# A sixth buffer for weight sets in a Strassen feed-forward, and the remainders' subtractions moved from GpSimd to VectorE

## The reference

```python
gate, up = split(h @ ffn_w_in, 2)          # ffn_w_in: 1024 x 5632
f = (silu(gate) * up) @ ffn_w_out          # ffn_w_out: 2816 x 1024
h = layer_norm(alpha * h + f)              # alpha = 4 ** 0.25
```

## Time and profile before

| | us |
|---|---|
| median of three runs | 2912.92 (2907.91 to 2914.14) |
| the profiled execution | 2908.02 |
| its span | 2906.2 |
| TensorE busy | 2577.3 (89%) |
| VectorE busy | 1685.0 (58%) |
| GpSimd busy | 1082.5 (37%) |
| ScalarE busy | 801.3 (28%) |
| sets' sums on GpSimd, L905, per block | 150.7 and 151.1 (x105 each) |
| sets' remainders on GpSimd, L908, per block | 136.1 and 136.2 (x105 each) |
| sets' remainders on VectorE, L779, per block | 41.9 (x42 each) |

### The profile page before, as it was taken

One profiled execution on the slowest core, in us unless ns is written; L12 is line 12 of the kernel. 1 busy time (PEld: TensorE's weight loads), 2 busy tenths in 40 slices (PEclk: granted clock), 3 DMA queues, 4 the chain that ended last, 5 costly groups with the idle time before them and its releaser, 6 DMA issues. The chain is left out here.

```text
span 2906.2 us, 40422 instructions
## 1 busy us (share of the span) xinstructions
PE 2577.3 (89%) x12972; PEld 2133.7 (73%) x12972; DVE 1685.0 (58%) x2971; ACT 801.3 (28%) x1363; POOL 1082.5 (37%) x810
## 2 busy tenths in 40 slices
PE   6787889699999999968999999995969999999995
PEld 5676678577777777757888888885857777777774
DVE  8789437645444454482667766666565444444447
ACT  3224232322222222213222222222132322222220
POOL 3979201545554544501011111100155545554450
PEclk9887999899999999989999999997989999999998
DMA  4333222244344333412110111102224434343341
GB/s 135 94 102 91 75 87 88 62 126 116 108 115 119 112 101 101 131 58 57 30 37 22 36 36 36 29 7 73 87 58 123 120 108 119 113 118 101 101 121 60
DMA packets 392575, 248.25 MB, mean 85 GB/s; under 512 B 24352, under 2 KB 374688, under 8 KB 391584
## 3 DMA queue, kind: packets, MB, share of 16 engines
q1 hardware_dynamic: 392480, 247.02, 28.9%
HBM read 229.20 MB, written 17.76 MB: 85 GB/s over the span
## 5 line engine op out<-in xcount | busy, mean ns | idle before, releaser
L835 DVE TENSOR_TENSOR h<-h,ps 128x512 f32<-128x512 f32 x320 | 219.4, 686 | 179.0 <-PE ps L498 178.9
L1977 POOL TENSOR_TENSOR w_lo<-w_raw_plain,w_hi 128x1024 fp32r<-128x1024 f32 x38 | 91.7, 2420 | 562.0 <-ACT w_hi L62 562.0
L2005 PE MATMUL ps<-aT_hi,w_hi 128*128 128x512 f32 x640 | 257.1, 402 | 1.7 <-PEq L324 1.7
L2005 PE MATMUL ps<-aT_hi,w_lo 128*128 128x512 f32 x640 | 251.7, 393 | 0.0
L2005 PE MATMUL ps<-aT_lo,w_hi 128*128 128x512 f32 x640 | 250.2, 391 | 0.0
L468 PE MATMUL ps<-aT_hi,s5o_w_sets 128*128 128x512 f32 x672 | 221.5, 401 | 28.0 <-DVE s5o_w_sets L779 20.0
L468 PE MATMUL ps<-aT_hi,hgo_w_sets 128*128 128x512 f32 x672 | 220.5, 399 | 28.4 <-DVE hgo_w_sets L779 20.0
L905 POOL TENSOR_TENSOR hgo_w_sets_plain<-hgo_w_sets_plain 128x512 f32<-128x512 f32 x105 | 150.7, 1436 | 177.3 <-DMA hgo_w_sets_plain<-in_ffn_w_in_dram 177.3
L905 POOL TENSOR_TENSOR s5o_w_sets_plain<-s5o_w_sets_plain 128x512 f32<-128x512 f32 x105 | 151.1, 1439 | 114.7 <-DMA s5o_w_sets_plain<-in_ffn_w_in_dram 114.7
L908 POOL TENSOR_TENSOR s5o_w_sets<-s5o_w_sets_plain,s5o_w_sets 128x512 fp32r<-128x512 f32 x105 | 136.2, 1297 | 132.5 <-ACT s5o_w_sets L62 131.6
L908 POOL TENSOR_TENSOR hgo_w_sets<-hgo_w_sets_plain,hgo_w_sets 128x512 fp32r<-128x512 f32 x105 | 136.1, 1296 | 131.0 <-ACT hgo_w_sets L62 131.0
(11 more groups left out here) (382 smaller groups left out, 6243.0 us busy)
## 6 DMA issues: line engine op xcount, KB each, us to landing
s5o_w_sets_plain<-in_ffn_w_in_dram SPq DMA_DIRECT2D x210, 256.0 KB, 3.3
hgo_w_sets_plain<-in_ffn_w_in_dram SPq DMA_DIRECT2D x210, 256.0 KB, 3.3
w_raw_plain<-in_hg_w_in_dram SPq DMA_DIRECT2D x40, 512.0 KB, 3.9
s5o_w_raw<-in_ffn_w_out_dram SPq DMA_DIRECT2D x22, 512.0 KB, 4.7
hgo_w_raw<-in_ffn_w_out_dram SPq DMA_DIRECT2D x22, 512.0 KB, 4.7
s5o_w_sets_plain<-in_ffn_w_in_dram SPq DMA_DIRECT2D x84, 128.0 KB, 2.3
hgo_w_sets_plain<-in_ffn_w_in_dram SPq DMA_DIRECT2D x84, 128.0 KB, 2.3
h<-in_x_dram SPq DMA_DIRECT2D x4, 1024.0 KB, 8.7
```

The lines of the kernel that those rows point to most:

```text
L835: v.tensor_tensor(to, to, ps[:, 4 + m % 4, :], ALU.add).then_inc(S["out_acc"], 1)
L1977: g.tensor_tensor(w_lo[b][:, :, :], w_raw[b][:, :, :], w_hi[b][:, :, :].bitcast(F32), ALU.subtract).then_inc(E[f"w_lo_done{b}"], 1)
L2005: ins = t.matmul(ps[:, half, :], w[b][:, kk, :], x[:, kk, cols], start=(kk == 0 and q == 0), stop=(kk == KT - 1 and q == 2))
```

## The change

- `SLOTS` is 6 and `SLOT_AT` is pos modulo 6. The norm's rows of gamma and beta lie in slots 4 and 5, before in 0 and 1.
- GpSimd makes only the sums (`make_sum`). VectorE makes all 14 remainders of an iteration (`set_lo`), and TensorE waits on one counter.
- `w2_raw` is gone. Both row blocks of `ffn_w_out` are loaded by one transfer of 1 MB straight into the memory of `w2_lo`, and the remainder is written in place. This load waits for the outputs before, whose operand it overwrites; it stands ahead of the iteration's set loads on SyncE.
- The hand-written orders of ScalarE, VectorE and GpSimd follow: `set_lo` calls stand between merges and between pairs of accumulations, and `w2_split` comes later in the iteration.

The diff (some context left out, deep lines moved left by eight columns):

```diff
@@ -160 +160 @@
-SLOTS = 5
+SLOTS = 6
@@ -210 +210 @@
-    w2_raw = sb("w2_raw", [P, D])
-    g_row, b_row = (plain_slots[:, n, :, :].rearrange("p h c -> p (h c)") for n in range(2))
+    w2_plain = in_rows(k.plain[tag + "_w2_lo"])
+    g_row, b_row = (plain_slots[:, n, :, :].rearrange("p h c -> p (h c)") for n in (4, 5))
-"set_in0", "set_in1", "set_in2", "set_in3", "set_in4", "set_sum", "set_hi", "set_lo", "set_lo_dve",
+"set_in0", "set_in1", "set_in2", "set_in3", "set_in4", "set_in5", "set_sum", "set_hi", "set_lo",
@@ -242 +242 @@
+    FIRST = range(NP, 2 * NP)
-    SLOT_AT = [0, 1, 2, 3, 4, 0, 1, 2, 3, 4, 0, 1, 2, 3]
+    SLOT_AT = [n % SLOTS for n in range(2 * NP)]
...
@@ -348 +345 @@
-    def load_w2(f):
-        if not (isinstance(f, int) and f == 0):
-            s.wait_ge(S["w2_lo"], f)
-            carry(s, f)
-        s.dma_start(w2_raw[:, :], w_out_v[:, ds(f, 1), :].rearrange("p f d -> p (f d)")
-                    ).then_inc(S["w2_loaded"], 16)
+    def load_w2(i):
+        if isinstance(i, int) and i == 0:
+            s.wait_ge(S["tile"], 2 * NT)
+        else:
+            s.wait_ge(S["out_tile"], i * NOUT)
+            carry(s, i)
+        s.dma_start(w2_plain, w_out_v[:, ds(2 * i, FG), :]).then_inc(S["w2_loaded"], 16)
@@ -368 +366 @@
     for half in range(2):
         tiles = slice(4 * half, 4 * half + 4)
         s.dma_start(h[:, tiles, :], residual_v[:, tiles, :]).then_inc(S[f"back{half}"], 16)
-    load_w2(0)
     s.wait_ge(S["w_lo"], 12)
-    for pos in range(NP, NP + 3):
+    for pos in FIRST[:3]:
         load_set(-1, pos)
     s.wait_ge(S["normed"], NT)
-    for pos in range(NP + 3, 2 * NP):
+    for pos in FIRST[3:]:
         load_set(-1, pos)
-    for pos in range(5):
+    load_w2(0)
+    for pos in range(SLOTS):
         load_set(0, pos)
 
     def body(i):
-        load_set(i, 5)
-        load_w2(2 * i + 1)
-        for pos in range(6, 2 * NP):
+        if not (isinstance(i, int) and i == 0):
+            load_w2(i)
+        for pos in range(SLOTS, 2 * NP):
             load_set(i, pos)
-        load_w2(2 * i + 2)
         if not (isinstance(i, int) and i == LAST - 1):
-            for pos in range(5):
+            for pos in range(SLOTS):
                 load_set(i + 1, pos)
 
     body(0)
@@ -397 +394 @@
-    load_w2(NF_LAST)
+    load_w2(LAST)
@@ -452 +449 @@
-            if IS_SUM[r]:
-                t.wait_ge(S["set_lo"], sums_to(i, pos))
-            else:
-                t.wait_ge(S["set_lo_dve"], plain_to(i, pos))
+            t.wait_ge(S["set_lo"], index(i, pos) + 1)
@@ -618 +612 @@
         keep_pair(pair)
     set_hi(-1, 10)
     set_hi(-1, 11)
+    set_hi(-1, 12)
     keep(0, 0)
     keep(0, 1)
-    set_hi(-1, 12)
+    set_hi(-1, 13)
     keep(0, 2)
-    set_hi(-1, 13)
     silu_late(0)
     set_hi(0, 0)
     silu_early(0)
-    for pos in range(1, 5):
+    for pos in range(1, SLOTS):
         set_hi(0, pos)
 
     def w2_split(i, q):
-        a.wait_ge(S["w2_loaded"], 16 * (2 * i + q + 1))
+        a.wait_ge(S["w2_loaded"], 16 * (i + 1))
         carry(a, i)
-        if isinstance(i, int) and i == 0:
-            a.wait_ge(S["tile"], 2 * NT)
-        else:
-            a.wait_ge(S["out_tile"], i * NOUT)
-            carry(a, i)
-        split_hi(a, w2_hi[:, q, :], w2_raw[:, :]).then_inc(S["w2_hi"], 1)
+        split_hi(a, w2_hi[:, q, :], w2_plain[:, q, :]).then_inc(S["w2_hi"], 1)
 
     def body(i):
         hidden_hi(2 * i, 0, i)
-        w2_split(i, 0)
         keep(2 * i + 1, 0)
         keep(2 * i + 1, 1)
-        set_hi(i, 5)
+        set_hi(i, 6)
+        set_hi(i, 7)
         keep(2 * i + 1, 2)
-        set_hi(i, 6)
-        w2_split(i, 1)
+        set_hi(i, 8)
         silu_late(2 * i + 1)
-        set_hi(i, 7)
+        set_hi(i, 9)
         silu_early(2 * i + 1)
-        set_hi(i, 8)
-        set_hi(i, 9)
+        w2_split(i, 0)
+        set_hi(i, 10)
         hidden_hi(2 * i + 1, 1, i)
+        set_hi(i, 11)
         keep(2 * i + 2, 0)
         keep(2 * i + 2, 1)
-        for pos in range(10, 13):
-            set_hi(i, pos)
+        w2_split(i, 1)
+        set_hi(i, 12)
+        set_hi(i, 13)
         keep(2 * i + 2, 2)
-        set_hi(i, 13)
         silu_late(2 * i + 2)
-        final = isinstance(i, int) and i == LAST - 1
-        if not final:
-            set_hi(i + 1, 0)
         silu_early(2 * i + 2)
-        if not final:
-            for pos in range(1, 5):
+        if not (isinstance(i, int) and i == LAST - 1):
+            for pos in range(SLOTS):
                 set_hi(i + 1, pos)
 
     body(0)
@@ -776 +762 @@
-        v.tensor_tensor(lo, plain_rows(pos)[1], hi.bitcast(F32), ALU.subtract).then_inc(S["set_lo_dve"], 1)
+        v.tensor_tensor(lo, plain_rows(pos)[1], hi.bitcast(F32), ALU.subtract).then_inc(S["set_lo"], 1)
-        v.tensor_tensor(w2_lo[:, q, :], w2_raw[:, :], w2_hi[:, q, :].bitcast(F32), ALU.subtract
+        v.tensor_tensor(w2_lo[:, q, :], w2_plain[:, q, :], w2_hi[:, q, :].bitcast(F32), ALU.subtract
@@ -844 +830 @@
         split_piece(1, kk)
     for n in range(NT):
         add_projection(0, n)
+    for pos in range(7, 10):
+        set_lo(-1, pos)
     for pair in range(PAIRS):
         for n in (2 * pair, 2 * pair + 1):
             add_projection(1, n)
@@ -851 +839 @@
         if pair >= 1:
             keep_pair(pair - 1)
     keep_pair(PAIRS - 1)
-    set_lo(-1, 10)
-    set_lo(-1, 11)
-    merge_steps(0, range(1, 11))
-    set_lo(0, 3)
-    set_lo(0, 4)
+    for pos in range(10, 13):
+        set_lo(-1, pos)
+    merge_steps(0, range(1, 5))
+    set_lo(-1, 13)
+    merge_steps(0, range(5, 11))
+    for pos in range(SLOTS):
+        set_lo(0, pos)
 
     def body(i):
+        merge_steps(2 * i + 1, range(1, 3))
+        set_lo(i, 6)
+        merge_steps(2 * i + 1, range(3, 5))
+        set_lo(i, 7)
+        merge_steps(2 * i + 1, range(5, 7))
+        set_lo(i, 8)
+        merge(2 * i + 1, 7)
+        set_lo(i, 9)
+        merge_steps(2 * i + 1, range(8, 10))
+        set_lo(i, 10)
+        merge(2 * i + 1, 10)
         split_w2(i, 0)
-        merge_steps(2 * i + 1, range(1, 5))
+        set_lo(i, 11)
+        merge_steps(2 * i + 2, range(1, 3))
+        set_lo(i, 12)
+        merge_steps(2 * i + 2, range(3, 5))
+        set_lo(i, 13)
         split_w2(i, 1)
-        merge_steps(2 * i + 1, range(5, 11))
-        set_lo(i, 10)
-        merge(2 * i + 2, 1)
-        set_lo(i, 11)
-        merge_steps(2 * i + 2, range(2, 11))
-        accumulate(i, slice(0, 4))
-        if not (isinstance(i, int) and i == LAST - 1):
-            set_lo(i + 1, 3)
-            set_lo(i + 1, 4)
-        accumulate(i, slice(4, NT))
+        merge_steps(2 * i + 2, range(5, 11))
+        final = isinstance(i, int) and i == LAST - 1
+        for two in range(PAIRS):
+            accumulate(i, slice(2 * two, 2 * two + 2))
+            if not final and two:
+                set_lo(i + 1, 2 * two - 2)
+                set_lo(i + 1, 2 * two - 1)
 
     body(0)
     with v.Fori(1, LAST - 1) as i:
@@ -897 +899 @@
-    def make_set(i, pos):
+    def make_sum(i, pos):
-        (hi, lo), (one, other) = set_rows(pos), plain_rows(pos)
+        one, other = plain_rows(pos)
-        g.wait_ge(S["set_hi"], index(i, pos) + 1)
-        carry(g, i)
-        g.tensor_tensor(lo, other, hi.bitcast(F32), ALU.subtract).then_inc(S["set_lo"], 1)
@@ -920 +919 @@
             g.tensor_tensor(hid_lo[:, q, HALF_COLS[half]], act_out[half][:, :],
                             hid_hi[:, q, HALF_COLS[half]].bitcast(F32), ALU.subtract).then_inc(S["hid"], 1)
 
-    for pos in range(NP, NP + 3):
-        make_set(-1, pos)
+    for pos in (7, 8, 9):
+        make_sum(-1, pos)
     for pair in range(PAIRS):
         pair_lo(pair)
-    make_set(-1, 12)
-    make_set(-1, 13)
-    for pos in range(3):
-        make_set(0, pos)
+    make_sum(-1, 12)
+    make_sum(-1, 13)
+    for pos in (0, 1, 2, 5):
+        make_sum(0, pos)
 
     def body(i):
         hidden_lo(2 * i, 0)
-        for pos in (5, 6, 7, 8, 9):
-            make_set(i, pos)
+        for pos in (6, 7, 8, 9):
+            make_sum(i, pos)
         hidden_lo(2 * i + 1, 1)
-        make_set(i, 12)
-        make_set(i, 13)
+        make_sum(i, 12)
+        make_sum(i, 13)
         if not (isinstance(i, int) and i == LAST - 1):
-            for pos in range(3):
-                make_set(i + 1, pos)
+            for pos in (0, 1, 2, 5):
+                make_sum(i + 1, pos)
 
     body(0)
     with g.Fori(1, LAST - 1) as i:
```

More of the change, by code:

```diff
@@ L282, in sums_to @@
         return f * NSUM + sum(IS_SUM[:r + 1])
-    def plain_to(i, pos):
-        f, r = tile_at(i, pos)
-        return f * (NP - NSUM) + r + 1 - sum(IS_SUM[:r + 1])
     def set_rows(pos):
```

## The result

| | before | after |
|---|---|---|
| median | 2913.45 (4 runs, 2907.91 to 2914.14) | 2818.32 (4 runs, 2816.45 to 2820.98) |
| the profiled execution | 2908.02 | 2817.46 |
| its span | 2906.2 | 2815.7 |

The ratio is 0.9678, with an interval of 0.9661 to 0.9695. 2824 had been predicted.

The account below looks back on a forecast made before the run. TensorE's feed-forward gaps, 89.0 us or 4.9 per iteration, were laid to late remainders: GpSimd's beat and one VectorE chain. 89.0 - 0.1 = 88.9 us off the median 2912.92 gave 2824, range 2814 to 2858 us.

Parts of the forecast that it names:

- The ceiling of 563.8 us: Each block's long feed-forward stage without gaps: ten outputs and nine times fourteen products, against 608.4 and 608.2 us measured before.
- the cost of 0 per iteration: New waits the change adds in each feed-forward iteration: between 0 and 4.9 us, taken as 0.
- It doesn't do what it says: Rival 4: the gaps move to other positions and nearly all stays, 2905 to 2915 us; chance 0.04.
- GpSimd's beat: GpSimd's 3.44 us per set, remainder to remainder, against TensorE's 2.75 us product, as cause of the iteration's gaps.
- The start of a block: Between unit -1 and body 0: a new 7.3 us stall plus 2.05 low clock; stage 69.1 us, no gain or loss.
- The megabyte: Output weights' 1 MB load at the iteration's start: through at 6.6 us, other bound 10.5, with set loads queued behind it.
- the narrowest place: Product 6 waiting for ScalarE's `keep` 2: ready at 15.2 us, wanted at 16.5, so 1.3 us to spare.
- The sign of 6 to 7 us from issue to landing: Sign that the prediction is right: `w2_lo` loads of 1 MB land 6 to 7 us after issue.
- the first rival: The megabyte lands late: no stall at 8.7 us; at 10.1, 1.1 us lost in 18 iterations, 2844 us; chance 0.12.
- The rule that spoke against the move: VectorE operations with two SBUF inputs and GpSimd ones exclude each other for a whole instruction; remainder 1.69 instead of 0.69 us.
- rivals 2 and 3: VectorE late by order, 1 us per unit: 2860, chance 0.09; slower, `keep` 2 late behind set 6's remainder: 2995, 0.05.
- Under 2.75: GpSimd without remainders: its beat per set falls from 3.44 to 1.29 us, under TensorE's 2.75 per product.

Follow-up runs that it names:

- two_megabytes: Changed kernel with the output weights loaded twice, 2 MB instead of 1 MB ahead of set 6: 2818.27 us, ratio 0.968 to the kernel before.
- lo_twice: Changed kernel with one more VectorE operation of a remainder's size ahead of each remainder: 2821.52 us, ratio 0.9688 to the kernel before.
- five_raw: Changed kernel with five slots and the output weights again by the raw tile, all remainders still on VectorE: 2883.39 us, ratio 0.9901 to the kernel before.
- orders_only: Kernel before with only the new hand-written orders, in effect the lists of ScalarE and VectorE: 2840.34 us, ratio 0.9763.
- gpsimd_rest: Changed kernel, six places kept, with the remainders of the summed sets given back to GpSimd: 2815.99 us, ratio 0.9673 to the kernel before.
- hi10_late: Changed kernel with five slots, summed sets' remainders on GpSimd, and sets 10 and 11 put back behind the keeps: 2906.35 us, ratio 0.9984 to the kernel before.
- hi10_early: Kernel before with set 10's rounding and remainder moved ahead of the end of the first tile: 2894.63 us, ratio 0.9947.

## Why the prediction was right

*The sum.* 88.9 us were predicted on the profiled execution, 90.6 measured (2908.02 - 2817.46). The median fell by 95.1, since that of after stands 0.9 above its profiled execution and not 4.9. The ceiling of 563.8 us from `outputs(0)` to the end of `outputs(9)` was met at 563.4 and 563.6, so the cost of 0 per iteration held. "It doesn't do what it says" is out: all four gaps of the earlier trace rows are gone. For the cause the number is no proof: the sum only took that all gaps go, and would have been the same with any other reason for them. That it held although one reason was wrong (GpSimd's beat, below) is luck.

*The start of a block.* Predicted 69.1 us, measured 68.77 and 67.84. The stall was 6.69 and 6.48 us where 7.3 stood, on the line named, and its low clock cost 1.9 where 2.05 stood. The gain of 1.5 in the first block goes with what the kernel before loses there: a stall of 3.18 us at 588.71 with 6 us at a granted clock of 0.50 behind it, against 2.28 us at 2191.60 with 4 us at 0.65 and 0.50 in the second.

*The megabyte.* The term was too large. Fitted to the queue of before, it was to be through 6.6 us into the iteration; issued at 0.25 and, by the page after, 5.0 to landing, it was there at 5.3. And set 6 did not queue behind it: issued at 2378.01, its sum started 4.07 us later, as set 5's did 3.96 after its issue in the earlier trace rows. So the sum of set 6 came at 7.04 instead of 8.8, and `keep` 2 ended at 13.56 instead of 15.2. The slack at the narrowest place was 2.9 us, not 1.3. The sign of 6 to 7 us from issue to landing did not come. Behind two megabytes, in `two_megabytes`, set 6 does queue: 6.78 us from issue to sum (2378.24 to 2385.02). With 2.0 us of the slack used up there almost nothing stalls, which fits. In the first rival 8.7 to landing moves everything by 2.5 and not 2.1, as the issue at 0.4 was left out; `keep` 2 would still be in time, at 16.1.

*VectorE.* The rule that spoke against the move is that a VectorE operation with two SBUF inputs contends with a GpSimd one that reads SBUF, in the Trainium skill (SBUF — State Buffer, Who interferes with whom). The trace agrees: 1.70 and 1.77 against 0.69. That VectorE has slack for it in the iterations is shown by `lo_twice`, where a whole further operation per set costs 3 us in all, no more than the noise. But `five_raw` shows that this depends on when things come: two splits in the first tile and a set 6 at 11.9 us (2240.48 - 2228.55) turn the same remainders into 71 us, clock included. The prediction gave rivals 2 and 3 0.14 together for the change as built, and asked for a late transfer to set them off; the runs bear both out.

*GpSimd's beat.* Here the reasoning failed though the number held. "Under 2.75" was the step: 3.44 us per set against a product of 2.75 looked like a rate that cannot keep up. But GpSimd has only ten such sets in an iteration and is idle for 15.96 us before its first instruction in it. Over the five sets in a row (5 to 9) it does fall behind by 0.7 us each, and where it starts late that shows at products 7, 8 and 9; where it starts earlier, in `orders_only`, only product 9 is still caught, and in `gpsimd_rest`, which has four in a row, none. So the start of the beat decided, and the rate alone was not the bound. `gpsimd_rest` keeps the beat and loses none of the gain; `orders_only` keeps beat and five places and has 71 of 95 us. The prediction had the order for one gap of the four, "the hi of set 10 now stands before `hidden_hi`", and it gave the other three to GpSimd. Of the 95 us, 71 come with the orders; what the three named parts do besides is 22 to 28, and not all are needed for it: with the output weights in place, either the sixth place or the remainders on VectorE is enough; without it, the remainders on VectorE lose 43 instead (2883 to 2840). Six places without it were not tried.

What stays open: how the 71 us split over the single moves. Sets 10 and 11 alone are 69 of 75 when taken out, with a longer stall and the low clock in it, and 20 when put in, with other gaps left, so the moves don't add up one by one.

## What to carry to other kernels

Where engines work fixed lists, look at what stands ahead of the late instruction in its list before pricing a gap by the rate of the engine that the profile names as releaser; compare that engine's load over the whole period before calling it the bound. Take an order apart by removing a move from the new version as well as adding it to the old: here one move was worth 69 us in the one direction and 20 in the other, because a gap that is closed uncovers the next, and because the stall that came back was longer and mostly had the low clock behind it. And a change with several parts may owe its gain to the one that its title doesn't name, so undo the titled parts all at once too, not only one by one.

## What the runs showed of the hardware

- Whether the low clock follows a stall of TensorE was not settled by the stall's length. In three windows of 2 us laid behind each, the granted clock fell after 14 of 16 stalls of 3.0 us (`hi10_late`), after 16 of 19 of 2.0 to 2.4 us (`five_raw`), but after only 2 of 16 of 2.03 us (before, once in a block: the earlier trace rows show one of the two), and after none of the 16 of 1.7 us in `hi10_early`. In one iteration of `hi10_late` product 10 waits 3.01 us, and the windows over it (columns as above) show the granted clock at 0.50, the lower of its two levels, with 48 matmuls in 12.64 us where 10.99 is usual; the expectation of 2875 was missed by this and by the length of the stall:

```profile
2328.00:2330.00 2.00, 0.81 (x2) 0.72 (x3) 1.64 (x3) 2.00 (x4) 0.00 (x0) 0.71 0.00 0
2330.00:2332.00 2.00, 2.00 (x6) 1.52 (x6) 0.86 (x2) 0.20 (x1) 1.62 (x2) 0.50 0.00 0
```
```profile
2329.19 12.64 PE ps L469 x48
```

- The output weights' 1 MB takes 5.0 us to land, the residual's 8.7: the size alone doesn't give the time.
- The mutual exclusion of VectorE and GpSimd also meets a merge with two SBUF inputs (1.77 us), while a merge with one input in PSUM stays at 0.69 beside a sum of GpSimd (2390.23 and 2390.29 above).
